# One of four channel tiles of a 31-tap depthwise filter: from VectorE to GpSimd, two operations per tap

## The chip, the cores and the metric

The kernel runs on one core of a Trainium2 chip. Its metric is the device time in microseconds (us) of one execution of the whole program; the median of three executions before the change is 2503.81 us (2501.68 to 2504.29). The engines are named as the profile names them: PE is TensorE's matmul, PEld its weight load, DVE VectorE, ACT ScalarE, POOL GpSimd, SP SyncE (here it only issues DMAs).

## The reference, cut to what matters

The program computes two transformer blocks for one sequence of 512 tokens: a first one with two branches (a convolution and a latent attention) and a convolutional feed-forward part, a second one with another attention, a delta-rule part and a mixture of experts. The change touches only the depthwise filter of the first block's convolution branch:

```python
def depthwise_conv(x, w, b):             # x (1, 512, 512 channels), w (31, 512)
    pad = k // 2
    y = lax.conv_general_dilated(x, w[:, None, :], window_strides=(1,), padding=[(pad, pad)],
        dimension_numbers=("NWC", "WIO", "NWC"), feature_group_count=c)
    return y + b

def conformer_conv(a, dw_w, dw_b, ln_g, ln_b, w_out, b_out):
    val, gate = a[..., :CONV_WIDTH], a[..., CONV_WIDTH:]
    u = val * jax.nn.sigmoid(gate)
    u = depthwise_conv(u, dw_w, dw_b)
    u = jax.nn.silu(layer_norm(u, ln_g, ln_b))
    return u @ w_out + b_out
```

The latent attention (`mla`) beside it has 8 heads, a query path (`q_c`, `w_uq`) and a key/value path (`kv_c`, `w_ukv`), and one rotated key part `k_rope` that all heads share. The two branches are added under gates after the filter's output has gone through its layer norm.

## The kernel before, in words

All activations are transposed: 128 channels lie on the partitions and the 512 tokens along the free dimension, in f32. The filter works on 512 channels, that is four channel tiles (`CT` = 4), and has 31 taps (`CK` = 31). Its input `u` is padded by 15 columns on each side; its output `cv` collects in place: tap j of tile t is `cv[t] = u[t][:, j:j+512] * w[j] + cv[t]`, one SCALAR_TENSOR_TENSOR of DVE with both tensors in SBUF (L717). Tap 0 is a TENSOR_SCALAR, which also adds the bias (L715).

Each engine runs its own list of instructions, written out by hand, and waits on semaphores. The order around the filter is this:

- PE multiplies the normed input by the gate and value columns (`cgate`, `cval`, L398), then by those of `qc`, `kvc` and the shared rotated key `kr`, then makes the eight query heads `uq` (which wait for `qn`), the keys `uk`, four tiles `v` (L438), and after these the attention: 32 steps of scores (L451), transposes (L458) and products (L467). The sum `cmean` over the filter's output (L481) stands behind the attention and waits for the filter.
- DVE writes `u` (L704), then the filter's first 12 taps in a row, then the norm of the query input (reciprocal L735, three products `qn` L670), the rotation of the shared key (L727, L728, L742), the norm of the key/value input (L744, two products L670). For each query head it then rotates the head (L727 and L728 read a PSUM bank; L753 adds two tensors in SBUF), which frees the head's PSUM bank, and does one tap of all tiles. The remaining 11 taps stand one in each second step of the attention, between the score maximum (L762), a copy of transposed probabilities (L769), the reciprocal (L774) and the scaling of the product (L778).
- POOL fills constants at the start and then only spreads the rotated key to the eight heads (L852, eight copies of 32 partitions, which wait for `kr_turned`); PE waits for these (`kr_spread`) ahead of the attention. After that POOL issues DMAs for the second block, once `mo` has been made, long after the filter.

PSUM has eight banks that the products use in turn. The four tiles of `v` need the banks of the query heads 4 to 7, so PE's L438 waits for DVE's L753. A step of attention waits for ACT's exponential (L597), which waits for DVE's maximum. A generator `taps` in `first_dve` hands out one tap (all channel tiles) at each `next(taps)`; `emptied_dve` and `emptied_act` count the PSUM banks that have been read.

Of the kernel before, what the change touches and what calls it, by code (L numbers as in the profile page):

```python
# [19 lines left out]
ALU = mybir.AluOpType  # L20
# [6 lines left out]
S = 512  # L27
# [3 lines left out]
CW, CK = 512, 31  # L31
CT = CW // P
HPAD = CK // 2
H1, NOPE, ROPE, VD = 8, 64, 32, 64
# [180 lines left out]
VECS = {}  # L215
# [141 lines left out]
X_, H_, BIG_ = 0, 4096, 8192  # L357
U_ = BIG_ + FT * S
CV_ = U_ + CT * (S + CK - 1)
# [17 lines left out]
def first_pe(c, pe):  # L377
    x, h = c.view(X_, DT, S), c.view(H_, DT, S)
    qn, kvn = c.view(C_, 3, S), c.view(C_ + 3 * S, 2, S)
    qT, kT, v = c.view(BIG_, H1, S), c.view(BIG_ + 4096, H1, S), c.view(BIG_ + 8192, TT, S)  # L380
# [3 lines left out]
    cv, mg, act = c.view(CV_, CT, S), c.view(BIG_, DT, S), c.view(BIG_, FT, S)  # L384
# [48 lines left out]
    for t in range(TT):  # L433
# [3 lines left out]
        for k in range(2):  # L437
            m = pe.matmul(bank, kvn[:, k, t * P:(t + 1) * P],  # L438
                          c.weight(c.plan.first["v", t] + 4 * k, 4), start=k == 0, stop=k == 1)
# [4 lines left out]
    for i in range(n + 2):  # L444
        if i < n:
            hd, t = i // TT, i % TT
# [6 lines left out]
        if 1 <= i <= n:  # L453
# [3 lines left out]
            for k in range(TT):  # L457
                m = pe.transpose(bank[:, k * P:(k + 1) * P], prob[:, (i - 1) % 2, k * P:(k + 1) * P], c.ident[:, :])  # L458
            m.then_inc(c.sem("job_done"), 1)
        if i >= 2:  # L460
            j = i - 2
# [4 lines left out]
            for k in range(TT):  # L466
                m = pe.matmul(bank[:, 0:VD], probT[:, j % 2, k, :], v[:, k, hd * VD:(hd + 1) * VD],  # L467
                              start=k == 0, stop=k == TT - 1)
            m.then_inc(c.sem("job_done"), 1)
    for t in range(TT):  # L470
# [3 lines left out]
        for j in range(TT):  # L474
            m = pe.transpose(bank[:, j * P:(j + 1) * P], o[:, t, j * P:(j + 1) * P], c.ident[:, :])
        m.then_inc(c.sem("job_done"), 1)
    pe.wait_ge(*c.bank_free("cmean", 0))
    bank = c.bank("cmean", 0)
    pe.wait_ge(c.sem("conv"), CT)
    for k in range(CT):  # L480
        m = pe.matmul(bank, c.ones[:, :], cv[:, k, :], start=k == 0, stop=k == CT - 1)  # L481
    m.then_inc(c.sem("job_done"), 1)
# [173 lines left out]
def first_dve(c, v):  # L656
    x, h = c.view(X_, DT, S), c.view(H_, DT, S)
    qc, kvc, kr = c.view(C_, 3, S), c.view(C_ + 3 * S, 2, S), c.view(C_ + 5 * S, S)
    qT = c.view(BIG_, H1, S)
    u, cv = c.view(U_, CT, S + CK - 1), c.view(CV_, CT, S)  # L660
# [47 lines left out]
    def conv_taps():  # L708

        for j in range(CK):  # L710
            for t in range(CT):
                w = VECS["conv_dw_w"][0] + t * CK + j
                w = c.vecs[:, w:w + 1]
                if j == 0:
                    v.tensor_scalar(cv[:, t, :], u[:, t, 0:S], w, c.vec("conv_dw_b", t), ALU.mult, ALU.add)  # L715
                else:
                    m = v.scalar_tensor_tensor(cv[:, t, :], u[:, t, j:j + S], w, cv[:, t, :], ALU.mult, ALU.add)  # L717
                    if j == CK - 1:
                        m.then_inc(c.sem("conv"), 1)
            v.drain()  # L720
            yield

    taps = conv_taps()

    def rotate(bank, out, scale):
# [32 lines left out]
    for i in range(n + 2):  # L758
# [4 lines left out]
        if 1 <= i <= n and i % 2 == 0:  # L763
            j = i - 1
# [5 lines left out]
        if i >= 2:  # L770
            j = i - 2
            hd, t = j // TT, j % TT
# [42 lines left out]
    for t in range(FT):  # L815
        for j, name in enumerate(("fg", "fu")):
            f = t + j * FT
            w = VECS["ffn_dw_w"][0] + 3 * f
# [27 lines left out]


def first_pool(c, g):
    kT, kr = c.view(BIG_ + 4096, H1, S), c.view(C_ + 5 * S, S)
    g.wait_ge(c.sem("kr_turned"), 1)  # L850
    for h in range(H1):
        g.tensor_copy(kT[64:96, h, :], kr[64:96]).then_inc(c.sem("kr_spread"), 1)  # L852

# [1678 lines left out]
def program(nc, plan, args):  # L2534
    with ExitStack() as ctx:
# [3 lines left out]
        @block.tensor  # L2539
        def _(pe):  # L2540
            first_pe(c, pe)
            second_pe(c, pe)
            experts_pe(c, pe)
# [17 lines left out]
        @block.gpsimd  # L2561
        def _(pool):
            constants_pool(c, pool)
            first_pool(c, pool)
            pool.wait_ge(*c.put_away("mo", DT - 1))
            modulation_pool(c, pool)
            second_pool(c, pool)
            route_pool(c, pool)
            experts_pool(c, pool)
            final_pool(c, pool)  # L2570
# [47 lines left out]
```

## Time and profile before

| | before |
|---|---|
| median of three executions | 2503.81 us |
| the profiled execution | 2502.6 us |
| its span | 2500.8 us |
| mean granted TensorE clock | 0.946 of full speed |
| busy share of PE / DVE / ACT / POOL | 89% / 32% / 18% / 5% |
| filter on DVE, taps 1 to 30 (L717) | 120 instructions, 82.1 us |

The span is the profile's own time from the first to the last instruction; 1.8 us of the execution lie outside it. The filter runs from 89 to 258 us of the span. A row of the time line gives the start of a group in us from the span's start, the time that it covers, the engine, the line, the operation with output and input, the shape and the count, and in brackets how long the engine had been idle before it and what ended this. Groups of equal instructions are merged to one row, so that 44 instructions in 30.87 us means one each 0.70 us. Shares of busy time over the whole span say little on a change in one stage of 200 us: that stage is read by itself.

### The profile page before, as it was taken

What the parts mean: (1) busy time and instruction counts of PE and PEld (TensorE: products, weight loads), DVE (VectorE), ACT (ScalarE), POOL (GpSimd) and SP (SyncE); (2) the same over time, 40 slices, a digit from 0 to 9 for tenths busy, and PEclk for the clock granted to TensorE, in tenths of its full rate; (3) what the DMA queues carried; (4) which work ended last, traced back from release to release, by engine and by line L of the source; (5) the groups of instructions that cost most, each with busy time, mean ns of one, the idle gap of its engine ahead of it and who ended that gap; (6) DMA issues with size and microseconds to landing.
All of it is one profiled execution on the core that took longest, in us unless ns stands there. A gap on an engine that the chain in (4) does not pass through costs nothing. (4 is left out here: it accounts for less than half of the span.)

```text
span 2500.8 us, 19716 instructions
## 1 busy us (share of the span) xinstructions
PE 2216.5 (89%) x7322; PEld 1073.9 (43%) x7322; DVE 792.4 (32%) x1486; ACT 449.1 (18%) x899; POOL 121.3 (5%) x201
## 2 busy tenths in 40 slices
PE   6988999999999999998899999999995687768773
PEld 2436644444444443544556496444445222222221
DVE  2587411034444201185436754100015010000004
ACT  1122400111111000124437262000011000000001
POOL 0000000000000000000102001000001000000002
PEclk9987999999999999999999999999995899989997
DMA  4217011314444222201011102122331799999996
GB/s 183 98 67 236 34 67 68 130 65 176 159 151 158 81 90 75 101 34 68 34 68 68 68 1 102 67 73 95 152 117 59 293 410 410 409 394 406 407 417 240
DMA packets 41835, 395.71 MB, mean 158 GB/s; under 512 B 6032, under 2 KB 6160, under 8 KB 21648
## 3 DMA queue, kind: packets, MB, share of 16 engines
q1 hardware_dynamic: 23328, 318.43, 32.6%
q0 software_dynamic: 13008, 50.86, 5.8%
q10 hardware_dynamic: 5408, 25.17, 3.1%
q8 instruction: 60, 0.98, 0.2%
q14 instruction: 31, 0.25, 0.0%
HBM read 375.57 MB, written 35.65 MB: 164 GB/s over the span
## 5 line engine op out<-in xcount | busy, mean ns | idle before, releaser
L398 PE MATMUL banks<-arena,ring 128*128 128x512 f32 x1856 | 806.4, 596 | 20.2 <-DVE arena L670 15.3
L1077 PE MATMUL banks<-arena,ring 128*128 128x512 f32 x1424 | 620.7, 596 | 7.6 <-ACT arena L1355 6.0
L398 PEld LDWEIGHTS banks<-arena,ring 128*128 128x128 f32 x1856 | 354.7, 191 | 469.6 <-issue 450.0
L1077 PEld LDWEIGHTS banks<-arena,ring 128*128 128x128 f32 x1424 | 270.6, 191 | 342.5 <-issue 338.3
L2182 PE MATMUL banks<-ring,arena 128*64 128x512 f32 x528 | 136.1, 666 | 55.7 <-DMA ring<-in_experts 37.6
L1350 ACT ACTIVATE arena<-banks 128x512 f32<-128x512 f32 (+5 forms) x151 | 77.6, 520 | 464.2 <-PE banks L1077 329.0
L2182 PE MATMUL banks<-arena 128*64 128x512 f32 x496 | 120.6, 633 | 44.5 <-DMA arena<-in_experts 36.9
L2406 DVE TENSOR_TENSOR arena<-arena,banks 128x256 f32<-128x256 f32 x32 | 13.5, 422 | 393.8 <-ACT arena L2372 393.8
L2182 PEld LDWEIGHTS banks<-ring,arena 128*64 128x64 f32 x528 | 41.8, 151 | 136.0 <-issue 89.1
L1174 PE MATMUL banks<-arena 128*128 128x128 f32 x768 | 92.0, 278 | 7.4 <-issue 6.9
L1174 PEld LDWEIGHTS banks<-arena 128*128 128x128 f32 x768 | 88.7, 193 | 9.4 <-issue 8.0
L2182 PEld LDWEIGHTS banks<-arena 128*64 128x64 f32 x496 | 36.8, 144 | 121.4 <-issue 74.2
L823 DVE SCALAR_TENSOR_TENSOR arena<-banks,vecs,arena 128x511 f32<-128x511 f32 x44 | 33.0, 749 | 159.9 <-ACT arena L647 159.9
L717 DVE SCALAR_TENSOR_TENSOR arena<-arena,vecs 128x512 f32<-128x512 f32 x120 | 82.1, 745 | 1.6
L647 ACT ACTIVATE arena<-banks,vecs 128x512 f32<-128x512 f32 x44 | 34.2, 778 | 263.3 <-PE banks L398 263.3
L2193 PE MATMUL banks<-arena 128*64 128x512 f32 x336 | 75.7, 592 | 0.8 <-issue 0.8
L1743 DVE SCALAR_TENSOR_TENSOR arena<-banks,vecs,arena 128x511 f32<-128x511 f32 (+2 forms) x72 | 53.8, 747 | 64.1 <-PE banks L1194 40.5
L2372 ACT ACTIVATE arena<-banks 128x256 f32<-128x256 f32 x32 | 12.3, 384 | 309.4 <-PE banks L2182 309.4
L1976 DVE CUSTOM_DVE_ANT_0 arena<-arena 128x1024 f32<-128x1024 f32 x48 | 58.7, 1222 | 3.4
L2200 PE MATMUL banks<-ident,arena 128*128 128x128 f32 x192 | 29.8, 289 | 32.9 <-DMA arena<-expert_rows 18.5
L2448 POOL DMA_DIRECT2D expert_results<-arena x64 | 34.0, 536 | 495.4 <-DVE arena L2424 495.4
L530 ACT ACTIVATE arena<-arena 128x512 f32<-128x512 f32 x28 | 17.2, 628 | 205.6 <-DVE arena L838 154.1
(314 smaller groups left out, 1680.5 us busy)
## 6 DMA issues: line engine op xcount, KB each, us to landing
ring<-in_stream SPq DMA_DIRECT2D x53, 2048.0 KB, 8.1
arena<-in_experts SPq DMA_DIRECT2D x52, 2048.0 KB, 31.1
ring<-in_experts SPq DMA_DIRECT2D x44, 2048.0 KB, 31.7
arena<-in_w_adaT POOLq DMA_DIRECT2D x48, 512.0 KB, 4.5
arena<-expert_rows ACTq DMA_DIRECT2D x64, 128.0 KB, 10.1
expert_results<-arena POOLq DMA_DIRECT2D x64, 128.0 KB, 7.7
arena<-in_xT SPq DMA_DIRECT2D x2, 1024.0 KB, 6.6
first_result<-arena POOLq DMA_DIRECT2D x1, 2048.0 KB, 6.6
```

What stands on the lines that cost most here:

```text
L398: m = pe.matmul(bank, c.weight(at + k), rhs(k), start=k == 0, stop=k == tiles - 1)
L647: a.activation(tmp[:, 2 * (t % 2) + j, :], bank, ACT.Identity, bias=c.vec("ffn_dw_b", f), scale=c.vecs[:, w + 1:w + 2]).then_inc(c.sem("mi ...
L717: m = v.scalar_tensor_tensor(cv[:, t, :], u[:, t, j:j + S], w, cv[:, t, :], ALU.mult, ALU.add)
L823: v.scalar_tensor_tensor(out[:, 1:S], bank[:, 0:S - 1], c.vecs[:, w:w + 1], out[:, 1:S], ALU.mult, ALU.add)
L1077: m = pe.matmul(bank, c.weight(at + k), rhs(k), start=k == 0, stop=k == tiles - 1)
L1174: return pe.matmul(out, lhsT, rhs, start=start, stop=stop)
L1350: a.activation(out, bank[:, 0:cols], func, **kw).then_inc(c.emptied("act", name, i), 1)
L1743: m = v.scalar_tensor_tensor(qkv[:, t, s:S], bank[:, 0:S - s], c.vecs[:, w + 3 - s:w + 4 - s], qkv[:, t, s:S], ALU.mult, ALU.add)
L1976: v.tensor_tensor_reduce(out=product, in0=bufs[:, i % 4, :], in1=row, scale=1.0, scalar=0.0, op0=ALU.mult, op1=ALU.add, accum_out=c.mod[:, ...
L2182: m = pe.matmul(out[side * SLOTS:(side + 1) * SLOTS], row, w[:, k, side, :], start=d == 0, stop=d == DT - 1)
L2193: m = pe.matmul(out[side * SLOTS:(side + 1) * SLOTS], row, w[:, f, side, :], start=f == 0, stop=f == 3)
L2448: g.dma_start(slot_rows(c.y_blocks, n)[side], c.view(YO_ + n % 3 * 512, 512)[side * SLOTS:(side + 1) * SLOTS]) \
```

## The change

DVE's filter covers three tiles instead of four. The fourth is computed by POOL, as 31 taps of the same sum. [...] POOL begins when `u` of tile 3 has been written and the vectors are there. The spreading of the rotated key is put after POOL's tap 15. PE's `cmean` waits for three filter tiles of DVE (`conv`) and one of POOL (`conv_last`).

```diff
@@ first_pe
-    pe.wait_ge(c.sem("conv"), CT)
+    pe.wait_ge(c.sem("conv"), CT - 1)
+    pe.wait_ge(c.sem("conv_last"), 1)
@@ first_dve, conv_taps
         for j in range(CK):
-            for t in range(CT):
+            for t in range(CT - 1):
@@ first_pool
-    g.wait_ge(c.sem("kr_turned"), 1)
-    for h in range(H1):
-        g.tensor_copy(kT[64:96, h, :], kr[64:96]).then_inc(c.sem("kr_spread"), 1)
+    t = CT - 1
+    g.wait_ge(c.sem("vectors"), 16)
+    g.wait_ge(*c.put_away("cval", t))
+    for j in range(CK):
+        w = VECS["conv_dw_w"][0] + t * CK + j
+        w = c.vecs[:, w:w + 1]
+        if j == 0:
+            m = g.tensor_scalar(cv[:, t, :], u[:, t, 0:S], w, c.vec("conv_dw_b", t), ALU.mult, ALU.add)
+        else:
+            now = c.view(BIG_ + 10240 + j % 2 * S, S)
+            g.tensor_scalar(now, u[:, t, j:j + S], w, None, ALU.mult)
+            g.drain()
+            m = g.tensor_tensor(cv[:, t, :], cv[:, t, :], now, ALU.add)
+        if j == CK - 1:
+            m.then_inc(c.sem("conv_last"), 1)
+        g.drain()
+        if j == CK // 2:
+            g.wait_ge(c.sem("kr_turned"), 1)
+            for h in range(H1):
+                g.tensor_copy(kT[64:96, h, :], kr[64:96]).then_inc(c.sem("kr_spread"), 1)
+            g.drain()
```

Two places show how the instructions stand. First POOL, from the end of its constants to its next DMA, before (`kr` is not named apart: `arena` is the one large SBUF tensor that holds nearly everything; `in_c` and `in_w_adaT` are inputs of the second block):

```order
L2528 MEMSET ones 128x128
L2530 ISA
L2530 AFFINE_SELECT ident<-ones 128x128
L852 COPY arena<-arena 32x512 x8
L1999 DMA arena<-in_c 128x1024
L2003 DMA arena<-in_w_adaT 128x1024 x48
```

and of the changed kernel (between the first and the second piece, and between the second and the third, the pair L862, L864 goes on):

```order
L2550 AFFINE_SELECT ident<-ones 128x128
L859 TENSOR_SCALAR arena<-arena,vecs 128x512
L862 TENSOR_SCALAR arena<-arena,vecs 128x512
L864 TENSOR_TENSOR arena<-arena 128x512
...
L862 TENSOR_SCALAR arena<-arena,vecs 128x512
L864 TENSOR_TENSOR arena<-arena 128x512
L871 COPY arena<-arena 32x512 x8
L862 TENSOR_SCALAR arena<-arena,vecs 128x512
L864 TENSOR_TENSOR arena<-arena 128x512
...
L2019 DMA arena<-in_c 128x1024
```

Sixty-one instructions have come to POOL: 31 of them stand ahead of the eight copies, 30 behind them. Second, DVE from the writing of `u` to the first query head's tap, before:

```order
L704 TENSOR_TENSOR arena<-banks,arena 128x512 x4
L715 TENSOR_SCALAR arena<-arena,vecs 128x512 x4
L717 SCALAR_TENSOR_TENSOR arena<-arena,vecs 128x512 x44
L735 RECIPROCAL arena<-arena 128x512
L670 SCALAR_TENSOR_TENSOR arena<-arena,vecs 128x512 x3
...
L753 TENSOR_TENSOR arena<-arena 32x512
L717 SCALAR_TENSOR_TENSOR arena<-arena,vecs 128x512 x4
```

and of the changed kernel, where every line from the filter on has moved down by one:

```order
L705 TENSOR_TENSOR arena<-banks,arena 128x512 x4
L716 TENSOR_SCALAR arena<-arena,vecs 128x512 x3
L718 SCALAR_TENSOR_TENSOR arena<-arena,vecs 128x512 x33
L736 RECIPROCAL arena<-arena 128x512
L671 SCALAR_TENSOR_TENSOR arena<-arena,vecs 128x512 x3
...
L754 TENSOR_TENSOR arena<-arena 32x512
L718 SCALAR_TENSOR_TENSOR arena<-arena,vecs 128x512 x3
```

The order on DVE is the same; each tap has one instruction less. PE's and ACT's instructions stand as they did.

## Rows read from the trace of the kernel before

**Rows 1.** The page's part 1: busy time, share and count of each engine.

```profile
PE 2216.5 (89%) x7322; PEld 1073.9 (43%) x7322; DVE 792.4 (32%) x1486; ACT 449.1 (18%) x899; POOL 121.3 (5%) x201
```

**Rows 2.** Stretches: length, then busy time (count) by engine, PE's clock, DMA.

```profile
133.00:162.00 29.00, 28.25 (x66) 12.16 (x64) 27.08 (x36) 9.68 (x17) 4.97 (x8) 1.00 0.20 72
162.00:182.00 20.00, 12.34 (x16) 3.78 (x16) 17.79 (x26) 2.33 (x5) 0.00 (x0) 0.67 0.00 0
...
197.00:213.00 16.00, 16.00 (x53) 11.44 (x53) 10.39 (x21) 3.68 (x9) 0.00 (x0) 0.50 0.92 292
213.00:244.00 31.00, 24.47 (x136) 16.98 (x137) 26.37 (x55) 9.39 (x25) 0.00 (x0) 0.94 0.74 235
...
258.00:285.00 27.00, 26.30 (x176) 20.44 (x176) 15.91 (x43) 12.03 (x30) 0.00 (x0) 1.00 0.00 1
```

**Rows 3.** Time line of DVE, 88 to 132 us: start, time covered, what.

```profile
88.33 0.69 DVE L704 TENSOR_TENSOR arena<-banks,arena 128x512 f32<-128x512 f32 x1 [13.04 <-PE banks L398]
89.12 1.91 DVE L715 TENSOR_SCALAR arena<-arena,vecs 128x512 f32<-128x512 f32 x4
91.11 30.87 DVE L717 SCALAR_TENSOR_TENSOR arena<-arena,vecs 128x512 f32<-128x512 f32 x44
126.03 3.35 DVE L735 RECIPROCAL arena<-arena 128x512 f32<-128x512 f32 x1 [4.05 <-ACT arena L537]
129.46 2.08 DVE L670 SCALAR_TENSOR_TENSOR arena<-arena,vecs 128x512 f32<-128x512 f32 x3
```

**Rows 4.** Time line of DVE, one query head and the tap behind it.

```profile
142.15 2.74 DVE L717 SCALAR_TENSOR_TENSOR arena<-arena,vecs 128x512 f32<-128x512 f32 x4
145.04 0.69 DVE L727 SCALAR_TENSOR_TENSOR arena<-banks,arena 32x512 f32<-32x512 f32 x1 [0.15 <-issue]
...
146.51 0.68 DVE L753 TENSOR_TENSOR arena<-arena 32x512 f32<-32x512 f32 x1
147.29 2.74 DVE L717 SCALAR_TENSOR_TENSOR arena<-arena,vecs 128x512 f32<-128x512 f32 x4
```

**Rows 5.** Time line of PE, from the query heads to the attention.

```profile
133.62 27.63 PE L398 MATMUL banks<-arena,ring 128*128 128x512 f32 x64
162.68 1.98 PE L438 MATMUL banks<-ring,arena 128*128 128x512 f32 x4 [1.43 <-DVE arena L753]
...
178.13 3.78 PE L438 MATMUL banks<-ring,arena 128*128 128x512 f32 x4 [1.36 <-DVE arena L753]
182.64 1.95 PE L451 MATMUL banks<-arena 96*128 96x512 f32 x4 [0.73 <-issue]
```

**Rows 6.** Time lines of DVE and PE, a tap in the attention at full clock.

```profile
233.00 2.73 DVE L717 SCALAR_TENSOR_TENSOR arena<-arena,vecs 128x512 f32<-128x512 f32 x4
...
237.50 0.63 PE L458 MATMUL banks<-ident,arena 128*128 128x128 f32 x4 [1.63 <-ACT arena L597]
```

**Rows 7.** Time lines of POOL and DVE, 134 to 139.9 us.

```profile
134.35 4.97 POOL L852 COPY arena<-arena 32x512 f32<-32x512 f32 x8 [130.83 <-DVE arena L742]
134.54 3.35 DVE L744 RECIPROCAL arena<-arena 128x512 f32<-128x512 f32 x1 [0.26 <-ACT arena L537]
...
137.69 0.61 POOL L852 COPY arena<-arena 32x512 f32<-32x512 f32 x1
137.98 0.86 DVE L670 SCALAR_TENSOR_TENSOR arena<-arena,vecs 128x512 f32<-128x512 f32 x1
138.25 1.07 POOL L852 COPY arena<-arena 32x512 f32<-32x512 f32 x1
138.76 1.09 DVE L670 SCALAR_TENSOR_TENSOR arena<-arena,vecs 128x512 f32<-128x512 f32 x1
```

**Rows 8.** Time line, 1524 to 1535 us: POOL's and DVE's instruction there.

```profile
1524.95 10.60 POOL L1960 TENSOR_SCALAR arena<-arena 128x4096 f32<-128x4096 f32 x1
1525.33 8.55 DVE L1838 SCALAR_TENSOR_TENSOR small<-small 128x32 f32<-128x32 f32 x1
```

**Rows 9.** Time line of POOL at the start: the instruction behind a drain.

```profile
3.22 0.29 POOL L2530 TENSOR_SCALAR_AFFINE_SELECT ident<-ones 128x128 f32<-128x128 f32 x1 [0.24 <-issue]
```

More of the change, by code:

```diff
@@ L848, in first_pool @@
 def first_pool(c, g):
+    u, cv = c.view(U_, CT, S + CK - 1), c.view(CV_, CT, S)
     kT, kr = c.view(BIG_ + 4096, H1, S), c.view(C_ + 5 * S, S)
-    g.wait_ge(c.sem("kr_turned"), 1)
-    for h in range(H1):
-        g.tensor_copy(kT[64:96, h, :], kr[64:96]).then_inc(c.sem("kr_spread"), 1)
+    t = CT - 1
[19 more added lines that the diff above has]
+            g.drain()
 HA, AD = 8, 128
```

## The prediction, made before the changed kernel was run

> **What bounds the kernel now.** I read the page's first part, then the stretches, then the time lines of DVE, PE and POOL around the filter. The page shows a kernel bound by PE (89%) in which DVE (32%) and POOL (5%) have room [rows 1]. That average does not hold where the filter runs. From 133 to 162 us DVE is busy for 27.08 of 29 us, and from 162 to 182 us for 17.79 of 20, while PE does only 12.34 us of work there and has its clock cut to 0.67 [rows 2]. The reader is to see three stages with three limits:
>
> - 89 to 132 us: the first 12 taps. DVE ends its 44 products at 91.11 + 30.87 = 121.98 and then idles for 4.05 us until ACT's root is there [rows 3]. The taps have 4 us of room.
> - 132 to 182 us: DVE is the bound. A query head costs 147.29 - 142.15 = 5.15 us of it, of which the tap is 2.74 [rows 4]. PE waits before each of the four tiles of `v` for DVE's L753, the last one at 178.13 [rows 5].
> - 182 to 258 us, the attention with 11 taps: at full clock PE stands still for 1.63 us behind a tap [rows 6]; at half clock (197 to 213) PE is busy all of the time [rows 2], and a shorter tap gives nothing. After the last tap, from 258 us, PE is busy for 26.30 of 27 us.
>
> **What goes.** One product in each tap, 30.87/44 = 0.70 us [rows 3]. In the first stage these are 11 x 0.70 + 0.48 = 8.2 us, all of it ahead of a wait, so worth nothing by itself: it raises the room from 4.05 to 12.3 us (the taps would end at 89.12 + 3 x 0.48 + 33 x 0.70 = 113.7; the root comes at 126.03). In the second stage 7 taps stand ahead of the last L753: 7 x 0.70 = 4.9 us. PE would not be late instead, since its 64 products end at 133.62 + 27.63 = 161.25 [rows 5] and the last tile would be wanted at 173. In the attention I count 7 of 11 taps at full clock: 4.9 us more, at most, as 1.63 us of wait are there to be taken [rows 6]. Together -9.8 us.
>
> **What comes.** 61 instructions on POOL, with 512 columns each on 128 partitions, begun at about 89 us and run beside DVE. POOL itself has time: `conv_last` is wanted at 285 us, and its eight copies by 182 us. The question is what DVE pays for them. Two places of the trace show POOL and DVE reading SBUF at once:
>
> - POOL's eight copies met two L670 of DVE. Undisturbed, three L670 take 2.08 us, 0.69 each [rows 3]; here the second took 1.09, and POOL's last copy took 1.07 where the one ahead of it took 0.61 [rows 7]. Each stood still for the other. The reciprocal beside the earlier copies, with one input, took its usual 3.35 [rows 3, 7], so only DVE's instructions with two SBUF inputs pay. One meeting with a copy cost 0.35 us.
> - POOL's TENSOR_SCALAR over 4096 columns held a DVE instruction of 32 columns for 8.55 us [rows 8]. That is 1.07 us for each 512 columns, of the very operation that the change makes 31 times.
>
> The Trainium skill has the rule behind this ("SBUF — State Buffer", section "Who interferes with whom"): the second SBUF port pair belongs to DVE and GpSimd together, one instruction holds it to its end, and a DVE instruction with two SBUF inputs needs it against a GpSimd instruction that reads SBUF. It speaks against this change, as all 90 remaining taps on DVE have two SBUF inputs; both places agree with it (1.09 and 8.55 us).
>
> Do they take turns strictly? POOL's own turn is 10.60/8 = 1.32 us for 512 columns [rows 8] and a drain adds 0.24 [rows 9], 1.56 together. DVE, held 1.07 and then running 0.70, needs 1.77, so POOL's next instruction is there before DVE's next one: each POOL instruction meets one of DVE. The margin of 0.2 us is thin; if it fails, DVE gets two instructions in a turn and pays about half as often in stage one.
>
> The price of a meeting: at least 0.35 (copy), 1.07 by the TENSOR_SCALAR; the TENSOR_TENSOR isn't in the trace, it reads twice as much, so between 0.35 and 2.14. I take 0.8 for all, nearer to the row of the same operation than to the copy, and lower than it because the 4096 columns are one long instruction and some turns will be missed.
>
> The sum with 0.8:
>
> - Stage one: 31 POOL instructions stand ahead of the wait for `kr_turned`, and DVE has 36 there. 113.7 + 31 x 0.8 = 138.5, against 126.03: the query norm is 12.5 us late, and all behind it on DVE. PE then waits for `qn` (about 10 us).
> - Between: POOL waits for `kr_turned`, then makes its copies beside the reciprocal and two L670, as it did before. No change. They end near 152, PE wants them after the last `v`.
> - Stage two: 30 POOL instructions beside the query heads. In a head L727 and L728 read PSUM (1.4 us, one POOL instruction passes free), the L753 and three taps have two SBUF inputs and meet four. Five in each round, so POOL's 30 last six rounds and 24 meet: 24 x 0.8 = +19.2 us, less the 4.9 of the shorter taps: +14.3.
> - Attention: POOL has finished by about 205, the last `v` starts at about 178 + 12.5 + 14.3 = 205 too. -4.9.
>
> 12.5 + 14.3 - 4.9 = +21.9 us. The profiled execution took 2502.6 us, so 2524.5; I say 2525. It lies 1.2 us below the median of the runs, which I leave out.
>
> Bounds by the same sum: at 1.07 it is 20.9 + 25.7 - 9.8 = +36.8, 2539; with TENSOR_TENSOR at 2.14 (a mean of 1.6) +66, 2569; at 0.35 it is 0 + 8.4 - 9.8 = -1.4, 2501. The change breaks even at 0.40 us for a meeting: 31p - 12.3 + 24p = 9.8.
>
> The Trainium skill says in the "GPSIMD Engine Reference", section 4.1, that one-input work on GpSimd runs at roughly line rate. The trace does not agree: 10.60 us for 4096 columns is 2.6 ns a column, where the copy's 0.61 us is 1.2 [rows 7, 8]. By that rule the TENSOR_SCALAR would cost a meeting what the copy did, and the mean of 0.35 and 1.07 is 0.71: 9.7 + 17.0 - 9.8 = +16.9, 2519.5. It is slower all the same, and inside the range.
>
> The clock adds noise. The half-clock stretch of 16 us, with PE busy throughout, would be 8 us of PE's work at full clock [rows 2], of which DVE's taps would take back a part; PE now idles in other places, and one such stretch more or less is about 4 us either way.
>
> **The rivals.**
>
> *DVE gets relief and pays nothing* (the other side). Place: the four waits of L438 and the 1.63 us behind each tap. For it: DVE is the bound from 132 to 182 us [rows 2, 5]. Against: both meetings in the trace. It gives the -9.8 alone, 2493, and decides as soon as a meeting costs well under 0.40 us.
>
> *Cheap meetings.* POOL's product and addition hold DVE no longer than a copy does, or DVE slips by in POOL's drains. For it: the 0.35 us [rows 7]; the 0.24 of a drain with POOL's own start in each gap. 2501 by the lower bound; up to 2509 it can't be told from no change. Against: the 8.55 us [rows 8].
>
> *POOL becomes the bound.* If an addition took 2.6 us and each instruction also waited for one of DVE (0.6), a tap would be 1.3 + 2.6 + 1.2 + 0.5 = 5.6 us and the last would end near 89 + 30 x 5.6 + 12.5 = 270 us, close to where `cmean` stands, with the stages late as by the price of 1.6. 2569 or more. For it: nothing but the missing row.
>
> **Chances.** DVE pays more than it gains, between about 2509 and 2560: 0.82, my forecast 2525. Relief alone 0.07. Cheap meetings 0.08. POOL the bound 0.03. Time differences of a measurement of this kernel can be told from nothing from about 0.2%, 5 us. So faster 0.08, the same 0.08, slower 0.84. The range runs from 2501 (price 0.35) to 2552 (price 1.3, POOL's own 1.32 us for a turn).
>
> **What would show it.** In the changed profile: L718 in stage one spaced by 1.3 to 1.8 us in place of 0.70, with single ones over 1 us; L736 starting near 138 in place of 126; L745 still 3.35; one query head costing 7 to 8.5 us of DVE while POOL works; PE's four L438 each waiting for DVE by more than before, the attention starting near 210 in place of 182.64; POOL's taps done between 190 and 230, and no wait of PE for POOL. In the attention PE's waits behind a tap fall from 1.63 to about 0.95. If L718 stays at 0.70 while POOL runs, the price is wrong and the time is 2493. If the attention starts by 187, the meetings are cheap. If it starts after 225, the addition is dearer than I took it.

## The result, and the profile after

The changed kernel takes 2511.28 us (median of 8 executions, 2507.78 to 2516.11) against 2503.90 for the kernel before (8 executions, 2501.68 to 2509.11), a ratio of 1.003 with a 95% interval of 1.0018 to 1.0043. It is slower, by 7.4 us (0.3%). I had forecast slower, by 21 to 22 us: right in direction, and the time lies inside the range, but the loss is a third of what I had summed.

The profiled execution took 2507.78 us with a span of 2506.1. The page's first part, to be set against [rows 1]:

```profile
PE 2205.9 (88%) x7322; PEld 1061.9 (42%) x7322; DVE 807.2 (32%) x1455; ACT 448.1 (18%) x899; POOL 217.5 (9%) x262
```

DVE has 31 instructions less and is busy for 14.8 us more: the instructions that are left have become longer. The time line of DVE (lines moved down by one), against [rows 3, 4]:

```profile
87.66 0.69 DVE L705 TENSOR_TENSOR arena<-banks,arena 128x512 f32<-128x512 f32 x1 [13.04 <-PE banks L398]
88.45 2.25 DVE L716 TENSOR_SCALAR arena<-arena,vecs 128x512 f32<-128x512 f32 x3
90.78 39.55 DVE L718 SCALAR_TENSOR_TENSOR arena<-arena,vecs 128x512 f32<-128x512 f32 x33
130.48 3.35 DVE L736 RECIPROCAL arena<-arena 128x512 f32<-128x512 f32 x1
133.90 3.52 DVE L671 SCALAR_TENSOR_TENSOR arena<-arena,vecs 128x512 f32<-128x512 f32 x3
...
171.50 0.69 DVE L729 SCALAR_TENSOR_TENSOR arena<-banks,arena 32x512 f32<-32x512 f32 x1
172.26 1.76 DVE L754 TENSOR_TENSOR arena<-arena 32x512 f32<-32x512 f32 x1
174.13 3.33 DVE L718 SCALAR_TENSOR_TENSOR arena<-arena,vecs 128x512 f32<-128x512 f32 x3
```

33 products now take 39.55 us, 1.20 each, where 44 took 30.87. L729, which reads PSUM, keeps its 0.69; L754 beside it, with both tensors in SBUF, takes 1.76. The reciprocal keeps its 3.35. Not every DVE instruction with one SBUF input gets off free, though: the three that make tap 0 (L716, TENSOR_SCALAR) cover 2.25 us where four took 1.91, as the second and third meet POOL's first two. The durations (min/median/max in ns), before and after:

```profile
L715 DVE TENSOR_SCALAR arena<-arena,vecs x4: 540/542/546, 89.1 to 90.5; 128x512 f32<-128x512 f32 x4
```

```profile
L716 DVE TENSOR_SCALAR arena<-arena,vecs x3: 560/917/935, 88.5 to 89.8; 128x512 f32<-128x512 f32 x3
```

Single instructions of DVE in stage one show how they meet POOL's, whose time line stands below them:

```profile
107.58 1.17 DVE L718 SCALAR_TENSOR_TENSOR arena<-arena,vecs 128x512 f32<-128x512 f32 x1
108.83 0.75 DVE L718 SCALAR_TENSOR_TENSOR arena<-arena,vecs 128x512 f32<-128x512 f32 x1
109.50 1.75 DVE L718 SCALAR_TENSOR_TENSOR arena<-arena,vecs 128x512 f32<-128x512 f32 x1
111.18 1.17 DVE L718 SCALAR_TENSOR_TENSOR arena<-arena,vecs 128x512 f32<-128x512 f32 x1
```

```profile
107.28 1.81 POOL L862 TENSOR_SCALAR arena<-arena,vecs 128x512 f32<-128x512 f32 x1 [0.17 <-issue]
109.24 1.47 POOL L864 TENSOR_TENSOR arena<-arena 128x512 f32<-128x512 f32 x1
110.88 1.81 POOL L862 TENSOR_SCALAR arena<-arena,vecs 128x512 f32<-128x512 f32 x1 [0.17 <-issue]
```

In a POOL cycle of 3.60 us (one product, one addition) DVE does three products: one that meets POOL's product takes 1.17, one that is held by neither 0.75, one that meets the addition 1.75. So a product costs DVE 0.42 us and an addition 1.00. POOL is held up too. Beside the reciprocal (130.48 to 133.83), which it doesn't meet, its product takes 1.56 and its addition 1.26:

```profile
130.82 1.26 POOL L864 TENSOR_TENSOR arena<-arena 128x512 f32<-128x512 f32 x1
132.25 1.56 POOL L862 TENSOR_SCALAR arena<-arena,vecs 128x512 f32<-128x512 f32 x1 [0.17 <-issue]
```

PE's time line, against [rows 5, 6]:

```profile
174.08 3.01 PE L438 MATMUL banks<-ring,arena 128*128 128x512 f32 x4 [3.03 <-DVE arena L754]
...
194.52 3.78 PE L438 MATMUL banks<-ring,arena 128*128 128x512 f32 x4 [3.84 <-DVE arena L754]
199.04 1.96 PE L451 MATMUL banks<-arena 96*128 96x512 f32 x4 [0.73 <-issue]
...
232.84 0.63 PE L458 MATMUL banks<-ident,arena 128*128 128x128 f32 x4 [0.97 <-ACT arena L598]
238.48 0.63 PE L458 MATMUL banks<-ident,arena 128*128 128x128 f32 x4 [0.97 <-ACT arena L598]
...
286.99 3.60 PE L482 MATMUL banks<-arena,ones 128*128 128x512 f32 x8
```

The attention begins at 199.04 in place of 182.64, and yet its end (L482, `cmean`) stands at 286.99 where it stood at 285.57. The attention itself, row by row of the stretches (the last figures are PE's granted clock, the DMA share and GB/s), first of the kernel before, then of the changed one:

```profile
182.64:285.57 102.93, 91.25 (x465) 66.38 (x465) 72.66 (x156) 34.46 (x84) 0.00 (x0) 0.83 0.52 164
```

```profile
199.04:286.99 87.95, 75.58 (x464) 54.52 (x465) 64.92 (x145) 33.98 (x84) 1.56 (x2) 1.00 0.60 192
```

PE does the same 465 products (one record is missing after) in 75.58 busy us in place of 91.25, because its clock was granted at 1.00 of full speed and not at 0.83. This is the largest thing that my sum lacked.

### The profile page after: what moved, and what is told of

It is laid out like the page before. It is cut to its first block and busy times, and to the rows that moved or that the text cites. A ratio compares the mean times of both kernels' runs of the same rounds, so it can differ in the third digit from the quotient of the medians.

```text
span 2506.1 us, 19809 instructions
## 1 busy us (share of the span) xinstructions
PE 2205.9 (88%) x7322; PEld 1061.9 (42%) x7322; DVE 807.2 (32%) x1455; ACT 448.1 (18%) x899; POOL 217.5 (9%) x262
## 5 line engine op out<-in xcount | busy, mean ns | idle before, releaser
L718 DVE SCALAR_TENSOR_TENSOR arena<-arena,vecs 128x512 f32<-128x512 f32 x90 | 87.8, 1029 | 1.6
L2023 POOL DMA_DIRECT2D arena<-in_w_adaT x48 | 25.4, 530 | 337.5 <-DVE modulation L1996 337.5
## 6 DMA issues: line engine op xcount, KB each, us to landing
arena<-in_experts SPq DMA_DIRECT2D x52, 2048.0 KB, 31.7
```

## The experiments

The edits are cut to what matters: where a run changes who makes a tap, the matching wait or signal (`conv`, `conv_last`) is changed with it and mostly not shown. All runs are compared by two lengths, read off each profile in the same way: L is from the start of DVE's last L704/L705 (the fourth tile of `u`) to the start of PE's last tile of `v`; A is from PE's first score product to `cmean`. These leave out shifts that a kernel brings from its start (the fourth tile of `u` is written at 87.35 to 89.82 us).

| kernel | median us | L us | A us | clock in A |
|---|---|---|---|---|
| before | 2503.9 | 89.80 | 102.93 | 0.83 |
| before, again (e1) | 2503.8 | 89.79 | 105.84 | 0.84 |
| changed | 2511.3 | 106.86 | 87.95 | 1.00 |
| changed, again (e9) | 2510.7 | 106.85 | 91.82 | 0.92 |
| relief (e2) | 2485.3 | 85.14 | 87.96 | 1.00 |
| burden (e3) | 2537.1 | 119.97 | 106.12 | 0.77 |
| writes (e4) | 2484.7 | 85.13 | 87.95 | 1.00 |
| products (e5) | 2489.7 | 88.33 | 87.93 | 1.00 |
| additions (e6) | 2499.9 | 95.18 | 87.95 | 1.00 |
| short attention (e7) | 2490.8 | 89.78 | 87.94 | 1.00 |
| moved, with POOL (e8) | 2501.1 | about 78 | 112.70 | 0.80 |
| first half (e10) | 2490.9 | 91.79 | 87.95 | 1.00 |
| spread only (e11) | 2495.3 | 89.79 | 92.36 | 1.00 |
| split tile (e12) | 2503.2 | 91.83 | 97.41 | 0.97 |

L repeats to 0.01 us in three pairs of runs; A repeats where the clock stays at full and moves by 3 to 4 us where it doesn't. For e8 L is an estimate, since PE makes its four tiles of `v` there without a wait between them (from 160.14 us, 7.03 us for all).

**Before and changed, again (e1, e9).** No edit. 

> The kernel before, unchanged, for a second profile of it. In its first profile the attention ran from PE's first L451 at 182.64 to L481 at 285.57 us, 102.9 us, with two stretches at half clock in it; in the changed kernel it took 88.0 us with none. Theory A (the clock gives part of the loss back): the half-clock stretches come from PE's idle time ahead of them, so they stand at the same places again and the attention takes 101 to 104 us. Theory B (chance): the stretches fall elsewhere from one execution to the next, and this profile's attention differs from 102.9 by 3 us or more.

> The changed kernel once more, for a second profile. In its first profile the attention starts at 199.04 us and takes 88.0 us with no half-clock stretch in it beyond its first 5 us. Theory A (short attention taps keep the clock up): attention within 1 us of 88 again. Theory B (chance): it differs by 3 us or more. The time 2507 to 2516 as before; the part of the loss that the first profile doesn't show (it is one of the fastest executions, 2507.8 against a median of 2511.3) lies behind the attention.

For e1 both theories were partly wrong: before's half-clock stretches do not stand at the same places again, but the mean clock of A is alike (0.83 and 0.84), and A differs by 2.9 us. For e9 theory B holds as it was written: A differs by 3.9 us, because one half-clock stretch, begun before the attention, this time reached into it (0.92). So A is noisy by 3 to 4 us. The difference between the two kernels is 11 to 18 us in these two profiles of each, and e7 and e11 below show it in whole runs.

**Relief without burden (e2).** The fourth tile's taps 1 to 29 are left out.

```diff
-    for j in range(CK):
+    for j in (0, CK - 1):
@@ the spreading of the key
-        if j == CK // 2:
+        if j == CK - 1:
```

> The changed kernel with taps 1 to 29 of the fourth tile left out (POOL does tap 0 and tap 30 only, then spreads the key). DVE has its relief and meets nearly no POOL instruction. Theory A (meetings on the shared read port are the whole loss): L718 at 0.70 us spacing throughout, attention starting 4.9 us earlier than before's 182.64 less 0.7, near 177; with 7 us of shorter taps and perhaps another 8 us of clock, 2485 to 2496 us. Theory B (the relief is worth nothing, because ACT or PE takes over as the limit): 2500 to 2505.

2485.32 us, ratio 0.9935 (0.9921 to 0.9949). The relief is worth 18.2 us, not my 9.8: 4.66 in L, as summed (4.9), and 15.0 in A, where I had 4.9 (the two of this one profile sum to 19.6).

**Burden without relief (e3).** DVE keeps four tiles, POOL works into scratch.

```diff
-            for t in range(CT - 1):
+            for t in range(CT):
@@ first_pool, tap 0 and the others
-            m = g.tensor_scalar(cv[:, t, :], u[:, t, 0:S], w, c.vec("conv_dw_b", t), ALU.mult, ALU.add)
+            m = g.tensor_scalar(c.view(BIG_ + 10752, S), u[:, t, 0:S], w, c.vec("conv_dw_b", t), ALU.mult, ALU.add)
-            now = c.view(BIG_ + 10240 + j % 2 * S, S)
+            now, out = c.view(BIG_ + 10240, S), c.view(BIG_ + 10752, S)
-            m = g.tensor_tensor(cv[:, t, :], cv[:, t, :], now, ALU.add)
+            m = g.tensor_tensor(out, out, now, ALU.add)
```

> DVE keeps all four tiles as before, and POOL does its 61 instructions beside it all the same, into scratch tiles that nobody reads. Cost without relief. Theory A: each POOL instruction costs DVE about 0.73 us where it meets one. Stage one: 44 instructions with the room of 4.05 us instead of 12.3; it takes 44 x 1.2 = 53 us in place of 31, so the query norm is 18 us late; stage two about 16 meetings or more at 0.6, so the attention starts 28 to 34 us later than before, near 213; the time is 2520 to 2540. Theory B (DVE's loss comes from its own shorter taps, for instance the drain behind three in place of four): the time stays within 5 us of before.

2537.12 us, ratio 1.0134 (1.0118 to 1.0150): 33.5 us, and L is 30.2 longer. POOL's instructions alone do it.

**Writes in place of reads (e4).**

```diff
-            g.tensor_scalar(now, u[:, t, j:j + S], w, None, ALU.mult)
+            g.memset(now, 1.0)
-            m = g.tensor_tensor(cv[:, t, :], cv[:, t, :], now, ALU.add)
+            m = g.memset(c.view(BIG_ + 10240 + (j + 1) % 2 * S, S), 1.0)
```

> The changed kernel with POOL's 60 products and additions replaced by 60 memsets of 128x512, which read nothing from SBUF; the taps 1 to 30 of the fourth tile are left out. Theory A (it is the read side that is shared, as DVE's taps have two SBUF inputs): L718 at 0.70 us throughout, time as in the relief run, 2485 to 2496. Theory C (any POOL instruction that touches SBUF holds DVE up, reads or writes): L718 spaced by over 0.9 us while POOL runs, attention starting 4 us or more later than in the relief run.

2484.71 us, ratio 0.9931 (0.9917 to 0.9945), as without POOL's work. DVE's products in this profile (min/median/max in ns) and POOL's memsets:

```profile
L718 DVE SCALAR_TENSOR_TENSOR arena<-arena,vecs x90: 740/746/753, 91.1 to 235.4; 128x512 f32<-128x512 f32 x90
```

```profile
L862 POOL MEMSET arena<- x30: 524/524/612, 90.1 to 157.1; 128x512 f32 x30
```

None of the 90 was held up, and 38 of them ran at the same time as one of the 60 memsets. It is POOL's reading of SBUF that DVE's two-input instructions wait for. DVE's TENSOR_SCALAR is another matter. The third L716 of this run met the first memset (and touched the second) and took 0.82 us in place of 0.54:

```profile
L716 DVE TENSOR_SCALAR arena<-arena,vecs x3: 560/820/915, 88.9 to 90.2; 128x512 f32<-128x512 f32 x3
```

That is one instruction in one profile; no run was made for it.

**One kind at a time (e5, e6).** Products alone, then additions alone (these add the unweighted input):

```diff
@@ e5
-            g.drain()
-            m = g.tensor_tensor(cv[:, t, :], cv[:, t, :], now, ALU.add)
@@ e6
-            g.tensor_scalar(now, u[:, t, j:j + S], w, None, ALU.mult)
-            g.drain()
-            m = g.tensor_tensor(cv[:, t, :], cv[:, t, :], now, ALU.add)
+            m = g.tensor_tensor(cv[:, t, :], cv[:, t, :], u[:, t, j:j + S], ALU.add)
```

> The changed kernel with POOL's additions left out: 30 products (TENSOR_SCALAR, one SBUF input) and a drain behind each, DVE with three tiles. In the changed kernel DVE's filter products run in a cycle of three: 1.76, 1.17 and 0.75 us. Theory A1 (the addition holds DVE for 1.02 us, the product only for about 0.42, as a copy does): no L718 over 1.3 us in stage one, and the time is 2486 to 2492, near the relief run's 2485.3. Theory A2 (both cost the same, 0.73, and the cycle comes from the drains): single L718 of 1.4 us or more, time about 2493 to 2498.

> The changed kernel with POOL's products left out: 30 additions (TENSOR_TENSOR, two SBUF inputs), which add the shifted input unweighted. Theory A1 (an addition costs DVE 1.02 us): L718 of 1.7 to 1.8 us appear in stage one, one for each addition; the attention starts at least 6 us later than in the relief run (177.68), and the time is 2492 to 2502. Theory A2 (same price for both): as the run with products alone, about 2493 to 2498, with no L718 over 1.5.

DVE's products in stage one, beside POOL's products, and beside its additions:

```profile
L718 DVE SCALAR_TENSOR_TENSOR arena<-arena,vecs x33: 737/752/1180, 91.3 to 119.5; 128x512 f32<-128x512 f32 x33
```

```profile
L718 DVE SCALAR_TENSOR_TENSOR arena<-arena,vecs x14: 1422/1588/1757, 92.3 to 112.9; 128x512 f32<-128x512 f32 x14
```

At most 1.18 us beside a product, up to 1.76 beside an addition. 2489.70 us and 2499.91: 4.4 and 14.6 more than the relief run. Together 19.0; the changed kernel has 26.0 more; there POOL works until 201 us, in these two until 167 and 165, so that it meets the last query heads too (a reason that no run tests by itself). An addition is dear, a product is not: theory A1 holds in both runs.

**The attention's taps alone (e7).** The kernel before; only in the attention the fourth tile is left out.

```diff
-            for t in range(CT):
+            for t in range(CT if j < 20 else CT - 1):
```

> The kernel before with one thing changed: the taps 20 to 30 (those in the attention) leave out the fourth tile on DVE; POOL does nothing new, and the first 20 taps have four tiles as before. It prices the attention's term alone. Theory A (shorter taps also keep PE's clock up): the attention starts at 182 to 183 us as before and takes 88 us, with no half-clock stretch of 10 us or more in it, so that the time is 2486 to 2492. Theory D (my forecast's term, shorter waits only, with the half-clock stretches staying): 4.9 us less, 2498 to 2500.

2490.75 us, ratio 0.9944 (0.9931 to 0.9957): 12.8 us for 11 products of 0.70. L is unchanged and A is 87.94, as in the changed kernel. The time line of PE in the kernel before shows two rates, two steps each at half clock and at full clock:

```profile
203.08 1.06 PE L458 MATMUL banks<-ident,arena 128*128 128x128 f32 x4
...
211.61 1.06 PE L458 MATMUL banks<-ident,arena 128*128 128x128 f32 x4
...
231.19 0.63 PE L458 MATMUL banks<-ident,arena 128*128 128x128 f32 x4 [1.63 <-ACT arena L597]
```

With the row at 237.50 [rows 6], two steps take 8.53 us at half clock (between the first two rows, with a group of the odd step left out) and 6.31 at full; in the changed kernel they take 238.48 - 232.84 = 5.64. Eleven blocks gain 11 x 0.67 = 7.4 us by the shorter tap at full clock, and what is left of the 15.0, 7.6 us, I put down to the half-clock stretches, which in these profiles come with the blocks of four. The stretch of e7's attention, to be set against the one of before above:

```profile
182.29:270.23 87.94, 75.58 (x465) 54.54 (x465) 64.90 (x145) 33.98 (x84) 0.00 (x0) 1.00 0.62 192
```

**First half only (e10).** POOL's taps 16 to 30 are left out, so that it rests from the spreading of the key on.

```diff
-    for j in range(CK):
+    for j in range(CK // 2 + 1):
```

> The changed kernel with POOL's taps 16 to 30 of the fourth tile left out, so POOL works beside stage one only and is idle from the spreading of the key on. It divides the loss between stage one and stage two. The relief run is 2485.3, the changed kernel 2511.3. Theory A: stage one is 5 us late as in the changed kernel, the query heads then run at 4.5 us each; 2489 to 2494, so that stage two is the larger part (17 to 22 us of the 26). Rival: stage one carries half or more, 2498 or more.

2490.90 us, ratio 0.9952 (0.9938 to 0.9965): the first half costs 5.6 us over the relief run, the second 20.4, as theory A had it.

**Three versions of the whole filter (e8, e11, e12).** e8 moves DVE's taps and POOL's work in time, e11 only regroups DVE's products of the kernel before, e12 halves the fourth tile between the engines.

```diff
@@ e8
-    for _ in range(12):
+    for _ in range(17):
@@ behind each query head
-        next(taps)
@@ first_pool
+    g.wait_ge(c.sem("qn"), 3)
-        if j == CK // 2:
+        if j == 5:
@@ e11, conv_taps of the kernel before
-        for j in range(CK):
-            for t in range(CT):
+        late = [(j, t) for j in range(20, CK) for t in range(CT)]
+        slots = [[(j, t) for t in range(CT)] for j in range(20)] + [late[i:i + 3] for i in range(0, len(late), 3)]
+        for slot in slots:
+            for n, (j, t) in enumerate(slot):
@@ e12, the changed kernel with POOL's taps 0 to 15 alone, and slots as in e11 from
+        late = []
+        for k in range(15):
+            late += [(20 + k, t) for t in range(CT - 1) if 20 + k < CK] + [(16 + k, CT - 1)]
```

> The whole filter again, on both engines as in the change, but put elsewhere in time: DVE does 17 three-tile taps in stage one (where it has room), none between the query heads, 14 in the attention; POOL begins only when the query norm is done (qn), and spreads the key after its tap 5. Theory A: stage one ends as before (L736 near 126), the v tiles come at PE's own pace and the attention starts at 168 to 172 in place of 182.64 or 199. In the attention POOL's instructions meet DVE's taps for about 65 us: 8 to 17 us given back there, and a risk of half-clock stretches. 2482 to 2497, so faster than both kernels. Theory E (POOL beside the attention costs as much as between the query heads): 2505 or more.

> The kernel before, POOL as before, with the whole filter on DVE; only the 44 products of the attention are dealt out three to a slot over 15 slots instead of four over 11. Nothing is computed elsewhere. Theory A (it is the length of a tap's block in the attention that decides PE's waits and its clock): the attention takes 90 to 95 us in place of 103, without half-clock stretches; 2493 to 2498, faster than both kernels. Rival (it was the number of products that mattered, not their grouping): 2501 to 2506, no change.

> The whole filter, with POOL computing taps 0 to 15 of the fourth tile (beside stage one, where DVE has room) and DVE its taps 16 to 30 in the attention, dealt out with the others three to a slot over 16 slots. Between the query heads DVE has three tiles and no POOL beside it. Theory A: stage one 5 us late, stage two 4.9 us shorter, attention 91 to 96 us; 2494 to 2501. If POOL's half is worth its price it beats the kernel that only deals the products out (e11, expected 2493 to 2498); I expect it doesn't.

e8: 2501.12 us, ratio 0.9984 (0.9976 to 0.9993), over my 2482 to 2497. The attention starts at 167.90, 14.7 us sooner than before, and then takes 112.70: POOL's instructions make a block of three products last up to 3.54 us, PE waits behind it, and its clock falls to 0.80. Its gain went there. A row of such a block, and PE's wait in another:

```profile
185.68 3.54 DVE L718 SCALAR_TENSOR_TENSOR arena<-arena,vecs 128x512 f32<-128x512 f32 x3
```

```profile
214.41 0.63 PE L458 MATMUL banks<-ident,arena 128*128 128x128 f32 x4 [2.42 <-ACT arena L598]
```

e11: 2495.32 us, ratio 0.9965 (0.9952 to 0.9979), faster than both kernels, with the whole filter on DVE. Fourteen blocks of three and one of two in place of eleven of four cost nothing in L and shorten A by 10.6 us, with the clock at 1.00.

e12: 2503.20 us, ratio 0.9997 (0.9988 to 1.0006), over my 2494 to 2501, with A at 97.41. Its attention keeps step with that of e11 for 79 us, and the other 5.05 us come at the end: the last two blocks hold three products each (2.23 and 2.39 us, a little over the 2.07 of the others, as one product of a tile waits for the other), where e11 has one block of two (1.40), and a half-clock stretch covers the last 5.4 us. PE's last wait in e12 and in e11:

```profile
273.79 0.63 PE L458 MATMUL banks<-ident,arena 128*128 128x128 f32 x4 [2.23 <-ACT arena L597]
```

```profile
270.49 0.63 PE L458 MATMUL banks<-ident,arena 128*128 128x128 f32 x4 [0.46 <-ACT arena L597]
```

## Why the prediction was right in direction and wrong in size

- *The mechanism held.* DVE's two-input instructions and POOL's instructions that read SBUF hold each other up (e3, e4); the reciprocal and the instructions that read PSUM don't meet POOL's. The Trainium skill's rule ("SBUF — State Buffer", "Who interferes with whom") says this, reads against two inputs and not writes, and both the 1.75 us beside an addition and the 753 ns at most beside a memset agree. But I had concluded that only two-input instructions of DVE pay, and that is too narrow: its TENSOR_SCALAR has one input and took 0.92 and 0.94 us beside POOL's. It cost 0.8 us in all here. That an instruction holds the port to its end, as my prediction gave the rule, does not show for POOL's product: in e8 one was under way from 131.76 us, POOL's next instruction began at 133.49, and between them L743 of DVE, with two SBUF inputs, ran from 132.65 in its usual 0.68 us. Nor does [rows 8] agree with it to the end: DVE's instruction was done at 1533.88, and POOL's by its record at 1535.55. The rivals of relief without a price and of POOL as the bound fell; `conv_last` came at about 201 us, well ahead of 287. The rival of cheap meetings was right on half of its ground, the product, and fell by the addition.
- *The price of a meeting, 0.8 us forecast, was about right:* (39.55 - 33 x 0.70)/23 = 0.71, from 0.42 and 1.00. My row for the product, 10.60 us for 4096 columns [rows 8], misled: a product of 512 columns holds DVE hardly longer than a copy (0.35, [rows 7]). For POOL's own time the row was the better guide: the product takes 1.56 us, 3.0 ns a column, so that the rule of the Trainium skill ("GPSIMD Engine Reference", section 4.1), one-input work at roughly line rate, does not fit this instruction, where a copy takes 1.2 ns a column. That the price worked out beside this rule, 0.71, is what was measured, is in part luck: it has the product at 0.35 (0.42 measured), but the addition at 1.07, a figure taken from a TENSOR_SCALAR (1.00 measured).
- *The step "do they take turns strictly?" failed.* I had POOL at 1.56 us an instruction and DVE held by each. Unhindered, POOL does take about that (1.71 for a product and 1.43 us for an addition, with the drain), but it is held up as well and takes 1.80, and a product holds DVE so briefly that two DVE instructions fit into its turn of 1.96 us: one of three is not held. In e6, with additions alone, the turns are strict. In stage one only 23 POOL instructions, not 31, met DVE's products: the reciprocal started 42.82 us behind L705 where it had been 37.70 behind L704, 5.1 late and not 12.5. The other eight ran beside the norm and the rotation and cost 0.6 us there (from the reciprocal to the first head's tap it is 16.76 us, after 16.12). Up to the last tile of `v` I had 26.8 us, and it was 17.1 (106.86 - 89.80); 7.4 of the 9.7 us between them are this first stage. A query head cost 6.82 us (L754 at 151.81 and at 158.63), a little under my 7 to 8.5; the 5.15 of before is a slip for 5.14, which changes nothing.
- *The term "attention, -4.9" failed, and is the larger miss.* It is 15.0 less by the first profile, 11.1 by e9 (91.82). The wait behind a tap fell to 0.97 us, as I had said (0.95). But I had counted 7 blocks at full clock, 0.70 each, and taken the half-clock stretches as given, with 4 us of noise. Those stretches go with the four-product blocks: they are in all three profiles with them (before, e1, e3; 0.77 to 0.84) while eight of the eleven with three to a block stand at 1.00. The other three differ: e9's stretch began before the attention, e8 has POOL beside it, and e12 has a short one at its very end, for which I have no cause. e7 and e11 change nothing but the blocks and have no stretch in A, so that the grouping is shown to matter; how the wait brings the clock down is not.
- *The sums.* By whole runs the relief is 18.2 us (e2), forecast 9.8; the burden on top of it 2511.3 - 2485.3 = 26.0, forecast 31.7. The two misses, 8.4 and 5.7, have the same sign in the total and make up my 21.9 against 7.4, but for 0.4 us. By the profiles L + A is +17.1 - 15.0 = +2.1, or +6.0 with e9; the rest up to 7.4 lies behind `cmean`, where the 14 profiles, with the same work there, differ by up to 8 us (2215.2 to 2223.6 us from `cmean` to the end), and I can't divide it further.

## What to carry to other kernels

An engine with idle time is no free helper if its instructions and those of the engine that it relieves hold each other up. Ask whether the helper's read SBUF, and whether the other's have two SBUF inputs, and price a meeting for each pair of instructions before counting relief: the long one of the same name did not give the price of the short one here. When an engine waits at regular intervals for another's block, the length of the block sets the wait, and here the clock's half-speed stretches came and went with it: dealing the same products out in threes gave 9 us (e11) with no second engine. Beside a stage whose clock is cut, neither take the cut as given nor count it as noise: it may go with the very wait that the change shortens.

## What the runs showed of the hardware that I had not expected

- GpSimd's product (TENSOR_SCALAR of 128x512, a multiplication alone) takes 1.56 us with nothing to meet and 1.81 where it meets two-input work of DVE, but holds such an instruction for 0.42; its TENSOR_TENSOR takes 1.26 with nothing to meet, up to 1.81 otherwise, and holds one for 1.00.
- The TENSOR_SCALAR of tap 0, which multiplies and adds, is much the shorter one: in e8, beside DVE instructions that read PSUM, it took 0.77 us, and the next instruction began 0.94 us after it, where the first product beside it took 1.58 and 1.73. No run separates the causes (the second operation, the other output, being the first), and no run tried the product in the form of tap 0.

```profile
130.82 0.77 POOL L859 TENSOR_SCALAR arena<-arena,vecs 128x512 f32<-128x512 f32 x1 [127.31 <-DVE arena L671]
131.76 1.58 POOL L862 TENSOR_SCALAR arena<-arena,vecs 128x512 f32<-128x512 f32 x1 [0.17 <-issue]
133.49 1.27 POOL L864 TENSOR_TENSOR arena<-arena 128x512 f32<-128x512 f32 x1
```

- 60 GpSimd memsets of 128x512, 0.52 us each as a rule: of the 38 two-input DVE instructions that ran beside one, none took over 753 ns. A DVE TENSOR_SCALAR with one SBUF input took 0.82 us beside them, where it takes 0.54 alone.
- Eleven DVE instructions of 0.70 us taken out of the attention gave back 12.8 us (e7), as TensorE's granted clock there rose from 0.83 to 1.00.
